# Up stage of the second block's MLP: weights as the stationary operand, and post norm's squares ahead of the next weights' pieces

## The reference

```python
def hybrid_layer(x, ...):
    ...
    mixed = jnp.concatenate([att, hm], axis=-1).astype(x.dtype)
    x = x + rms_norm_2(mixed @ w_out, g_mix_post)

    u = rms_norm_2(x, g_mlp_pre) @ w_up          # 1024 -> 4096
    u = jnp.square(jax.nn.relu(u))
    x = x + rms_norm_2(u @ w_down, g_mlp_post)   # 4096 -> 1024
    return x
```

## Time and profile before

| | us |
|---|---|
| median of three runs | 1856.5 |
| lowest and highest run | 1856.46, 1861.02 |
| span of the profiled execution | 1859.4 |

### The profile page before, as it was taken

How to read it: one execution, slowest core, us unless ns; L and a number is a source line. 1 busy time by engine, 2 the same in 40 slices (tenths; PEclk the granted TensorE clock), 3 DMA queues, 4 the chain that set the end, 5 groups by cost and what they waited for, 6 DMA issues and landing times.

```text
span 1859.4 us, 25694 instructions
## 1 busy us (share of the span) xinstructions
PE 1843.4 (99%) x8848; PEld 1550.7 (83%) x8848; DVE 1397.7 (75%) x1556; ACT 1199.8 (65%) x1344; POOL 160.6 (9%) x184
## 2 busy tenths in 40 slices
PE   9999999999999999999999999999999999999998
PEld 8998888888888888888888888888888888878887
DVE  6666476546677888888888888888889896587653
ACT  6544365437765777677777776777778766666542
POOL 3000000004404400000000000000001221000000
PEclk9999999999999999999999999999999998999999
DMA  9655655554339999999999999999999963445550
GB/s 293 189 179 212 195 181 182 184 198 139 136 129 339 343 395 395 395 395 392 394 395 397 393 394 383 379 385 370 391 376 369 395 259 103 136 148 162 179 197 29
DMA packets 237863, 516.19 MB, mean 278 GB/s; under 512 B 15260, under 2 KB 55312, under 8 KB 237792
## 3 DMA queue, kind: packets, MB, share of 16 engines
q1 hardware_dynamic: 232304, 499.70, 75.0%
q0 software_dynamic: 5184, 14.51, 2.2%
q10 hardware_dynamic: 304, 1.05, 0.2%
HBM read 506.78 MB, written 8.42 MB: 277 GB/s over the span
## 4 chain that ended last, share of the span: by engine, by line
PE 96%; DVE 2%; ACT 1%; issue 0%; DMA 0%; ACTq 0%; DVEq 0%; SPq 0%
PE G L1525 24%; PE G L1527 24%; PE G L1526 24%; PE SM L1527 5%; PE SM L1525 5%; PE SM L1526 5%; PE T L1485 3%; PE T L1929 1%; DVE e_low L718 1%; PE SM L1713 1%; PE G L1796 1%; PE SM L1814 0%; PE SM L1770 0%; PE SM L2073 0%; PE G L1914 0%
## 5 line engine op out<-in xcount | busy, mean ns | idle before, releaser
L718 DVE TENSOR_TENSOR e_low<-e_arrived,e_high 128x2048 fp32r<-128x2048 f32 (+1 forms) x346 | 759.0, 2248 | 86.9 <-ACT e_high L710 86.9
L710 ACT CAST e_high<-e_arrived 128x2048 fp32r<-128x2048 f32 x338 | 624.4, 1913 | 4.8 <-PE SM L1527 4.8
L1525 PE MATMUL G<-e_high,work_r 128*128 128x512 f32 x896 | 353.8, 395 | 1.2 <-DVE e_low L718 0.8
L1527 PE MATMUL G<-e_high,work_r 128*128 128x512 f32 x896 | 349.4, 390 | 0.0
L1526 PE MATMUL G<-e_low,work_r 128*128 128x512 f32 x896 | 348.6, 389 | 0.0
L1525 PE MATMUL G<-dense_high,xT_hi_all 128*128 128x512 f32 (+1 forms) x760 | 295.4, 389 | 1.7 <-ACT work_all L1118 0.7
L1527 PE MATMUL G<-dense_high,xT_lo_all 128*128 128x512 f32 (+1 forms) x760 | 284.1, 374 | 0.0
L1526 PE MATMUL G<-dense_low,xT_hi_all 128*128 128x512 f32 (+1 forms) x760 | 283.1, 373 | 0.0
L492 DVE TENSOR_TENSOR dense_low<-dense_raw,dense_high 128x2048 fp32r<-128x2048 f32 (+1 forms) x73 | 148.0, 2056 | 89.5 <-ACT dense_high L474 88.1
L1527 PEld LDWEIGHTS G<-e_high,work_r 128*128 128x128 f32 x896 | 168.1, 188 | 35.9
L1525 PEld LDWEIGHTS G<-e_high,work_r 128*128 128x128 f32 x896 | 168.3, 188 | 35.4 <-DVE e_low L718 1.7
(11 more groups left out here) (370 smaller groups left out, 2085.9 us busy)
## 6 DMA issues: line engine op xcount, KB each, us to landing
e_arrived<-in_m_w_in_dram SPq DMA_DIRECT2D x448, 512.0 KB, 8.4
e_arrived<-in_m_w_out_dram SPq DMA_DIRECT2D x224, 512.0 KB, 8.2
dense_raw<-in_a_w_in_dram SPq DMA_DIRECT2D x32, 768.0 KB, 6.0
dense_raw<-in_f_w_in_dram SPq DMA_DIRECT2D x44, 512.0 KB, 4.7
dense_raw<-in_w_up_dram SPq DMA_DIRECT2D x16, 1024.0 KB, 5.1
dense_raw<-in_w_down_dram SPq DMA_DIRECT2D x16, 1024.0 KB, 4.9
dense_raw<-in_a_w_out_dram SPq DMA_DIRECT2D x12, 1024.0 KB, 5.1
dense_raw<-in_f_w_out_dram SPq DMA_DIRECT2D x11, 1024.0 KB, 4.9
```

Source lines behind the costliest of these rows:

```text
L710: nc.scalar.copy(e_hi_unit(n), e_raw(n, e_arrived)).then_inc(e_hi, 1)
L718: ins = nc.vector.tensor_tensor(e_raw(n, e_low)[:, at], e_raw(n, e_arrived)[:, at], e_hi_unit(n)[:, at].bitcast(F32), ALU.subtract)
L1525: nc.tensor.matmul(bank, x_hi, w_hi, start=start, stop=False)
L1527: return nc.tensor.matmul(bank, x_lo, w_hi, start=False, stop=stop)
```

## The change

The up stage turns its operands round, from slab 1 on. The weights become the stationary operand, and the tokens stream: for each of four blocks of 128 hidden columns and each of the 8 chunks, one product of the high weights with 512 columns (256 low and 256 high tokens, fetched as a pair from two places, `x_pair`) and one of the low weights with the 256 high tokens. The bank of a block then holds two halves, and the hidden values lie with hidden columns on the partitions, as the down stage reads them; nothing is turned. DVE adds the two halves of a bank (`block_sum`, a reduction out of PSUM over pairs), ACT takes relu and two squares of a pair of blocks, one plain and one rounded (`held_high`), and DVE subtracts for the low part (`held_low`). Slabs alternate between two sets of four banks (`held_bank`). Slab 0 stays as it was and is still turned, in slab 1. The norm's factor is no longer applied at relu: it is positive, so it passes through relu, and its square and fourth power are put into the last norm (`in_scale2`, `in_scale4`). The down stage waits for low parts of pairs instead of turns.

In the joint, ACT's squares of tile 0 go ahead of unit 1's pieces, the gain's DMA behind them; the squares of tile 1 and their root go ahead of unit 2's pieces; the second tile is turned before its square. The mean is folded into the squares' scale, so `post_norm` has one step less. On DVE, unit 0's low parts go ahead of the second mixed low half, and unit 1's are cut in two around the low turn. On PE the second tile's turns stand inside the last products of tile 0, and `keep_busy` is gone there.

The diff, cut to its core:

```diff
+        def x_pair(k):
+
+            one = x_both[:, k * S:(k + 1) * S]
+            return bass.AP(one.tensor, one.offset, [one.ap[0], [x_gap, 2], [1, S]])
...
+        def held_bank(s, j):
+
+            return (G[2:4] + SM if s % 2 else G[0:2] + T)[j]
+
+        block_sums = [xn[:, 0, b * BANK:(b + 1) * BANK] for b in range(2)]
+        block_squares = [xn[:, 1, b * BANK:(b + 1) * BANK] for b in range(2)]
...
-            def post_norm_squares(full, c, meanwhile=None):
+            def post_norm_squares(full, c):
...
-            make_high(act, mu.first + 1)
             base = pr_base + len(TURN2_NO)
             act.wait_ge(att2.out_full, UNITS2)
+            post_norm_squares(12, 0)
+            make_high(act, mu.first + 1)
             act.dma_start(post_gain2, t["g_mlp_post_2"].to_broadcast([P, D])).then_inc(post_landed[1], 16)
-            post_norm_squares(12, 0)
             high_turn(turned2, base, 0, None)
-            post_norm_squares(12, 1, lambda: make_high(act, mu.first + 2))
+            post_norm_squares(12, 1)
+            make_high(act, mu.first + 2)
+            high_turn(turned2, base + 2, 1, None)
             square(0, 16 + 2)
-            high_turn(turned2, base + 2, 1, None)
             make_high(act, mu.first + 3)
             square(1, 16 + 4)
             take_root(1)
             take_root(1)
             base += 4
...
-            def relu(s, c):
-                n = 2 * s + c
-                act.wait_ge(mu.full, n + 1)
-                if s:
-                    act.wait_ge(relu2_ready, n - 1)
-                else:
-                    act.wait_ge(rstd_ready, 10 + c + 1)
-                nc.scalar.activation(xn[:, c, 0:BANK], G[2 * (s % 2) + c][:, :], ACT.Relu, scale=rstd[:, c:c + 1]).then_inc(mu.done, 1)
-
-            for s in range(mu.slabs):
-                if s:
-                    make_slab(make_high, act, mu, s + 1, md)
-                for c in range(NT):
-                    if s:
-                        hidden_high(turned2, base + 2 * (s - 1) + c, s - 1, c, 4)
-                for c in range(NT):
-                    relu(s, c)
+            def relu(c):
+                act.wait_ge(mu.full, c + 1)
+                nc.scalar.activation(xn[:, c, 0:BANK], G[c][:, :], ACT.Relu).then_inc(mu.done, 1)
+
+            def held_high(s, pair):
+
+                n = 2 * (s - 1) + pair
+                act.wait_ge(mu.done, 2 + 2 * n + 2)
+                steps.then(nc.scalar.activation(block_sums[n % 2], block_sums[n % 2], ACT.Relu))
+                if n >= 2:
+                    act.wait_ge(block_low, n - 1)
+                nc.scalar.activation(block_squares[n % 2], block_sums[n % 2], ACT.Square)
+                k = 4 * s + 2 * pair
+                nc.scalar.activation(hT_hi_all[:, k * S:(k + 2) * S], block_sums[n % 2], ACT.Square).then_inc(split_copied, 1)
+
             for c in range(NT):
-                hidden_high(turned2, base + 2 * (mu.slabs - 1) + c, mu.slabs - 1, c, 4)
+                relu(c)
+            for s in range(1, mu.slabs):
+                make_slab(make_high, act, mu, s + 1, md)
+                if s == 1:
+                    for c in range(NT):
+                        hidden_high(turned2, base + c, 0, c, 4)
+                for pair in range(2):
+                    held_high(s, pair)
             rest_high(md)
             for c in range(NT):
...
                         w_hi, w_lo = high_place(n), low_place(n)
                         pe.wait_ge(tc[part], base // 2 + c + 1)
                         for kk in range(4):
+                            if late == 2 and c == 0 and part and kk >= 2:
+                                other_tile(kk - 2)
                             k = 4 * part + kk
...
-            def second_tile2():
-                keep_busy(SM[0], 8)
-                added_turns2(16, base, 1)
-                keep_busy(SM[0], 8)
-
-            split_first(mu, tc, base, second_tile2, late=1)
+            def second_tile2(j):
+                tile_turns(tf, tc, base, 1, 16, (j,))
+
...
+            def held_slab(s):
+
+                for part in range(2):
+                    n = mu.first + 2 * s + part
+                    split_ready(n)
+                    w_hi, w_lo = high_place(n), low_place(n)
+                    for j in range(4):
+                        bank = held_bank(s, j)
+                        if part == 0:
+                            bank_free(s, j)
+                        for kk in range(4):
+                            k = 4 * part + kk
+                            at = slice(kk * BANK + j * P, kk * BANK + (j + 1) * P)
+                            nc.tensor.matmul(bank[:, :], w_hi[:, at], x_pair(k), start=(k == 0), stop=False)
+                            ins = nc.tensor.matmul(bank[:, S:2 * S], w_lo[:, at], xT_hi[:, k, :], start=False, stop=(k == KD - 1))
+                        if part:
+                            ins.then_inc(mu.full, 1)
+                    if part == 0:
+                        ins.then_inc(mu.half_used, 1)
+                        if s == 1:
+                            slab_before(squared_turn, 1, base)
+            split_first(mu, tc, base, second_tile2, late=2)
             base += 4
             for s in range(1, mu.slabs):
-                split_use(mu, s, lambda: slab_before(squared_turn, s, base))
...
+            make_low(dve, mu.first)
             mixed_low_half(1)
-            make_low(dve, mu.first)
...
-                dve.wait_ge(post_landed[nth - 1], 16)
                 with_gain(0)
                 dve.wait_ge(post_squares, 4 * (nth - 1) + 2 * c + 2)
-                steps.then(V.tensor_tensor(ss[:, c:c + 1], ss4[:, 2 * c:2 * c + 1], ss4[:, 2 * c + 1:2 * c + 2], ALU.add))
                 roots[0] += 1
-                V.tensor_scalar(var, ss[:, c:c + 1], 1.0 / D, EPS, ALU.mult, ALU.add).then_inc(variance_ready, 1)
+                if nth == 1:
+                    V.tensor_scalar(var, parts[0], parts[1], EPS, ALU.add, ALU.add).then_inc(variance_ready, 1)
...
+            make_low(dve, mu.first + 1, (0, 1))
             low_turn(tc, 0, None)
-            make_low(dve, mu.first + 1)
+            make_low(dve, mu.first + 1, (2, 3))
...
-            def relu_squared(s, c, base):
-                n = 2 * s + c
-                dve.wait_ge(mu.done, n + 1)
-                if s:
-                    dve.wait_ge(tf, base + n - 1)
+            def relu_squared(c):
+                dve.wait_ge(mu.done, c + 1)
                 V.tensor_tensor(xn[:, c, BANK:2 * BANK], xn[:, c, 0:BANK], xn[:, c, 0:BANK], ALU.mult).then_inc(relu2_ready, 1)
 
-            for s in range(mu.slabs):
-                if s:
-                    make_slab(make_low, dve, mu, s + 1, md)
-                for c in range(NT):
-                    if s:
-                        hidden_low(tc, s - 1, c, 4)
-                for c in range(NT):
-                    relu_squared(s, c, base)
+            def block_sum(s, j):
+
+                n = 4 * (s - 1) + j
+                dve.wait_ge(mu.full, 2 + n + 1)
+                bank = held_bank(s, j)
+                V.tensor_reduce(block_sums[n // 2 % 2][:, n % 2 * S:(n % 2 + 1) * S],
+                                bank[:, :].rearrange("p (b n) -> p n b", b=2), AX_X, ALU.add).then_inc(mu.done, 1)
+
+            def held_low(s, pair):
+
+                n = 2 * (s - 1) + pair
+                high_parts[0] += 1
+                dve.wait_ge(split_copied, high_parts[0])
+                k = 4 * s + 2 * pair
+                V.tensor_tensor(work_r[:, k * S:(k + 2) * S], block_squares[n % 2], hT_hi_all[:, k * S:(k + 2) * S].bitcast(F32),
+                                ALU.subtract).then_inc(block_low, 1)
+
             for c in range(NT):
-                hidden_low(tc, mu.slabs - 1, c, 4)
+                relu_squared(c)
+            for s in range(1, mu.slabs):
+                make_slab(make_low, dve, mu, s + 1, md)
+                if s == 1:
+                    for c in range(NT):
+                        hidden_low(tc, 0, c, 4)
+                for j in range(3):
+                    block_sum(s, j)
+                held_low(s, 0)
+                block_sum(s, 3)
+                held_low(s, 1)
```

More of the change, by code:

```diff
@@ L243, in build @@
         dense_high = place(HIGH * UNIT, RAW * UNIT, "dense_high", F32R)
-        xT_lo_all = place(KD * S, 12 * UNIT, "xT_lo_all", F32R)
         xT_sum_all = place(KD * S, 13 * UNIT, "xT_sum_all", F32)
@@ L435, in consumed @@
                     eng.wait_ge(down_full, ph.downs + 4)
+            elif ph is mu and u % 2:
+                eng.wait_ge(mu.full, 2 + 4 * (u // 2))
             elif u % 2:
@@ L1508, in norm_turns, with tile_turns @@
                     turn(tf, tc, base + j, [src[:, c, k * P:(k + 1) * P] for k in (2 * j, 2 * j + 1) for c in range(NT)])
-            def tile_turns(tf, tc, base, c, ready=None):
-                for j in range(2):
+            def tile_turns(tf, tc, base, c, ready=None, halves=range(2)):
```

(43 more changed lines are left out.)

15 lines of the change are left out of this document (9 added, 6 removed).

## The result

| | before | after |
|---|---|---|
| median, us | 1856.66 (6 runs) | 1865.34 (6 runs) |
| lowest and highest run | 1856.45, 1861.17 | 1864.78, 1869.49 |
| span of the profiled execution | 1859.4 | 1863.3 |

The changed kernel is slower: the ratio is 1.0046, with a 95% interval of 1.0034 to 1.0058, that is 8.7 us. Predicted were 1866.0 us and a range of 1859.5 to 1873.5.

What follows compares the result with a forecast made beforehand. PE bounds the kernel before; after, ACT and DVE waiting for each other, 14.1 us a slab against PE's 11.09. Summed 9.2 to 9.4 us longer; 1856.5 + 9.5 = 1866.0 us, range 1859.5 to 1873.5.

Steps and rivals of the forecast that it cites:

- The round: Up stage: ACT and DVE wait for each other in program order, 14.1 us a slab against 11.09 on PE.
- The price that no row had shown: DVE's sum of a bank's two halves out of PSUM: 0.69 us, 0.60 from start to start.
- both bounds: Limits for one DVE sum out of PSUM: 0.48 us below, 1.22 us above if read at half pace.
- PE's pace: Up stage from slab 1 on: 256-column products 0.120 us apart, so a slab takes PE 11.09 us, 0.70 less.
- the rival with dear products: 256 columns cost PE as much as 512: a slab 14.5 us, 1873 us; chance 0.06 together with the clock's.
- the rival in which PE keeps the pace: ACT and DVE need under 11.1 us a slab, so the gain of 8.1 us stands: 1848.4 us; chance 0.06.
- The lead: Pieces ready ahead of PE run out at slab 3, where PE waits 1.6 us and starts at 1703.7.
- The joint: Before the up stage's slab 0: tile 1's products start at 1673.5 instead of 1676.74, 3.2 us gained.
- PE's waits: Start of slabs 4 to 7: PE waits for DVE's low pieces, about 3 us each.
- The rival of the clock: PE's clock falls after the new waits; at most the last wait's 2.5 us show, 1868.5; chance 0.06 with dear products.

Runs made afterwards that it cites:

- the order was changed: Changed kernel with slab 2's pieces made first, then one unit of slab s + 2 between the pairs of slab s on ACT and DVE: 1848.59 us.
- the moved sum: Changed kernel with DVE making the sum of block 3 before the low part of pair 0 instead of behind it: 1855.33 us.
- the filled waits: Changed kernel with sixteen identity transposes on PE ahead of its wait at the start of slabs 3 to 7: 1867.95 us.
- the kernel with the up stage alone: Changed kernel with the joint's steps put back in their old order, the new up stage kept: 1867.95 us.
- the squares on the ring: Changed kernel with two more squares, results unused, on ACT in each slab from 2 on, ahead of the next slab's eight pieces: 1872.93 us.
- the kernel with the pieces a slab earlier: Changed kernel with all eight pieces of slab s + 2, not s + 1, in one block ahead of slab s's sums and squares: 1864.63 us.

## Why the prediction was right, point by point

**The round** is the term that decides, and each of its steps came out to within 0.02 us:

| step | predicted | measured |
|---|---|---|
| ACT's first four pieces | 2.59 | 1709.46 - 1706.88 = 2.58 |
| DVE's eight pieces | 5.30 | 1700.66 - 1695.36 = 5.30 |
| two sums | 1.33 | 1701.98 - 1700.66 = 1.32 |
| relu and two squares, pair 0 | 1.84 | 1703.83 - 1701.98 = 1.85 |
| low part, sum of block 3 | 1.33 | 1705.16 - 1703.83 = 1.33 |
| relu and two squares, pair 1 | 1.70 | 1706.88 - 1705.16 = 1.72 |
| round | 14.1 | 14.10 |

The price that no row had shown, the sum of two halves out of PSUM, is 0.68 us alone and 0.60 from start to start, as L2519's reduction; both bounds were wide of it.

**PE's pace.** 256 columns take 0.12 us from start to start behind 512 at 0.23, as on the line of the earlier trace rows (timeline of after, PE):

```profile
1680.99 0.40 PE L2227 MATMUL G<-x_both,dense_high 128*128 128x512 f32 x1
1681.23 0.28 PE L2228 MATMUL G<-x_both,dense_low 128*128 128x256 f32 x1
1681.34 0.39 PE L2227 MATMUL G<-x_both,dense_high 128*128 128x512 f32 x1
```

A slab takes 11.09 us where nothing waits. So the rival with dear products falls, and the rival in which PE keeps the pace was right on its price: 1848.4 us predicted, 1848.59 measured once the order was changed. It needed only what the change doesn't do, pieces that are made while something else waits. That the round stands because a queue is worked off in its order was read from the earlier trace rows. The prediction set beside it that the Trainium skill (TensorE: Matmul & The Clock Gate, section Architectural detail) calls the queues of ScalarE and VectorE strictly first in, first out; the moved sum, worth 10.0 us without any work saved, agrees with it.

**The lead.** The places lie 0.3 us early up to slab 1, and about one microsecond early from ACT's pieces of slab 2 on (times of after with 4.59 added):

| | predicted | measured |
|---|---|---|
| tile 1's first product of slab 0 | 1673.5 | 1673.25 |
| slab 1 | 1679.0 | 1678.71 |
| ACT's pieces of slab 2 | 1683.0 | 1682.05 |
| slab 3 | 1703.7 | 1702.74 |
| slab 7 | 1760.1 | 1759.16 |
| down stage | 1773.1 | 1772.21 |
| its third unit | 1785.8 | 1784.71 |

The mis-sized term is the way from the joint to the ring's first turn: 0.95 us of it lie ahead of slab 2's pieces, and of these 0.5 ahead of the end of unit 3's low parts (1680.1 predicted; 1672.30 + 2.74 + 4.59 = 1679.63), the rest in the two roots and slab 0's relus. Against before the third unit is 1784.7 - 1776.6 = 8.1 us late, not 9.2. Behind it stand 0.35 us that the prediction gave no price: 0.16 in the last norm, which from PE's last product on takes 7.07 us (1856.23 to 1863.3) instead of 6.91, and 0.19 between the third unit's start and that product. Together 8.5 us in the trace and 8.7 by the medians, with 9.5 predicted. Of the 9.5, the prediction's own places give 9.2 (1785.8 - 1776.6); for the 0.3 us above that it names no term.

**The joint** gains 3.5 us on PE (1676.74 - 1673.25), where 3.2 were worked out; alone it gives 3.7 of time.

**PE's waits** at slabs 4 to 7 were put at 3.0 us each. They are 2.74, 1.01, 2.54 and 1.17 us: two come near, two are far below. In this kernel the clock fell after both long waits, the slab behind took PE 1.4 to 1.7 us longer, and the next wait was shorter by that. The rival of the clock was therefore right that it falls, and the prediction was right that in the round it costs nothing: the filled waits showed it. That idle stretches of PE bring the lower clock back is also a rule of the Trainium skill (TensorE: Matmul & The Clock Gate, Part 1: The HAM clock gate); the waits here agree with it in part, as the last section tells.

## What to carry to other kernels

Two engines that each work in order and hand results to each other form a ring; its length is the sum of the steps along the waits, and it can set the pace while every engine in it has a third of its time free. Add up one turn of it before counting busy time, and look for the place where the other work of both engines, put between the steps, covers the waits: here the same instructions in another order moved the time from 1865.3 to 1848.6 us. Starting that other work earlier, without putting it between, left the ring as long as it was (14.10 us) and the time nearly so (1864.6 us).

## What the hardware showed that was not expected

That the granted clock falls after single waits of 2.0 us and more in a stage where PE is otherwise busy without a gap was left open in the prediction; that the length of the wait alone doesn't decide it was not expected. In the kernel with the up stage alone PE waited 2.74, 2.55, 2.73 and 2.54 us ahead of slabs 4 to 7, and only after the last did the clock fall (PE's busy time, clock, DMA share, GB/s; slabs 4, 5 and 7):

```profile
1719.83:1723.83 4.00, 4.00 (x23) 1.00 0.47 180
...
1733.94:1737.94 4.00, 4.00 (x23) 1.00 0.45 184
...
1762.15:1766.15 4.00, 4.00 (x15) 0.64 0.41 168
```

With the squares on the ring it fell after a wait of 2.02 us (0.58 in the four microseconds behind it) and not after one of 2.50 (1.00). In the up stage waits of 0.7 to 1.2 us were followed by no fall in any kernel here. What else decides, no run shows. In the ring a fall was free; behind the wait of 3.95 us in the kernel with the pieces a slab earlier it cost about 2.9 us, because there PE was the last. And the clock at the gates is 0.50 for some ten microseconds in some executions and 1.00 in others: it was 0.50 in all four profiled executions out of the upper group of a kernel's times, and 1.00 in the other six. Where a kernel's runs fall into two groups, these lie some 4.5 us apart.
